# A fifth buffer of gathered rows in the residual's place, masks laid down before the scores, and two side products moved

## The chip, the cores and the metric

The kernel runs as one program on one core of a Trainium2 chip. The time is the device time of one execution in microseconds (us). Before the change it is 2636.42 us, the median of 3 runs (2633.18 to 2641.44). Five engines work side by side and wait for each other by semaphores: TensorE (PE: matmuls and transposes into PSUM; its weight loads are shown as PEld), VectorE (DVE), ScalarE (ACT), GpSimd (POOL) and SyncE (SP). Here SP issues the loads of weights and POOL the gathers and stores.

## The reference, cut to what matters

Two layers of a decoder for 512 prompt tokens and 8 sampled sequences of 4 tokens. The sampled tokens attend over a paged cache of 2048 old rows per sequence, in three branches that share the queries:

```
kv_c, ends = compress_kv(cmp_all, w_cmp1, w_cmp2)        # blocks of 32 rows -> one key and value
o_cmp, p_cmp = cmp_attend(q, kv_c, ends, q_pos, ...)     # softmax over the compressed blocks
idx = select_blocks(p_cmp, q_pos, n_keys)                # top 16 of 33 blocks of 64 rows
o_slc = sel_attend(q, idx, q_pos, blocks, slopes)        # softmax over rows of the selected blocks
o_win = win_attend(q, keys, q_pos, k_pos, slopes)        # softmax over the last 512 rows
o_a = ga[0] * o_cmp + ga[1] * o_slc + ga[2] * o_win
x = x + mix @ w_out                                      # x: the residual, needed again only here
```

A softmax score is `q.k - slope * distance`, with blocked rows at minus infinity. The rest of a layer (input projection, prompt attention, gated linear attention, mixing, ConvFFN) is not touched.

## The kernel before, in words

All is in fp32. The residual rows lie turned in SBUF (`xT`, 128 x 8 x 544) for the whole program. In a layer the normed rows `hT` are made from `xT`; after that `xT` is not read until the products `wo0` to `wo7` are added to it (DVE, L2189), some 700 us into a layer of 1300 us.

Past rows come in pieces of 2 MB, one for each sequence and branch (128 partitions x 16 rows x 256 numbers). POOL issues them (`gather`, L687; `window`, L695) into `XSLOTS` = 4 buffers, taken in turn in the order of `XSTEPS`: `cmp0` to `cmp8`, `win0`, `slc0` to `slc3`, `win1`, `slc4` to `slc7`. A piece may start when the last user of the piece four places earlier is done (`x_slot_free`). So `slc3` takes the buffer of `win0` and waits for its last product (`ow0`), `win1` takes that of `slc0` and waits for the last product of the first half (`os0`), and `slc7` takes that of `win1` and waits for `ow1`. POOL's queue is in order: whatever stands behind a waiting gather waits too.

Sampled attention is done in two halves of 4 sequences, each one PE, DVE and ACT in turn:

- window: keys turned (L989), scores (L996), mask distances added and the maximum taken (DVE), exponentials (ACT), probabilities turned (L1007, L1008), times values (L1015, L1019);
- selected rows: keys turned in four steps (L1057), each copied out of PSUM by ACT and DVE, scores in four steps (L1068) into two PSUM pairs `ss..0` and `ss..1`; DVE adds the distances `dslc` to each pair (1024 wide), then over all 2048 the selection mask `selml`, takes the maximum over 2080, ACT takes exponentials over 2080, PE turns the probabilities (L1086, L1090), and multiplies by the values (L1100, L1104).

Where a softmax chain runs, PE is given a piece of the input projection that needs nothing from it, 32 matmuls of 272 columns at L790: a side product. `side_steps` says where: `("s", 0, 2)` (`qb0`) behind the first window scores, `("s", 0, 0)` (`qb1`) behind the first half's selected scores, `("s", 1, 1)` (`kb0`) ahead of the second window, `("s", 1, 0)` (`kb1`) behind the second half's selected scores. DVE copies each out of PSUM. PE and DVE use two PSUM pairs in turn (`T0`, `T1`) for turned tiles and side products.

## Time and profile before

| | |
|---|---|
| runs, median (lowest to highest) | 2636.42 us (2633.18 to 2641.44) |
| profiled execution, own time | 2633.0 us |
| its span | 2630.7 us |
| PE busy | 2474.3 us, 94% of the span |
| DVE busy | 794.6 us, 30% |
| ACT busy | 525.1 us, 20% |
| mean granted clock of PE | 0.957 of full speed |

PE is the busiest engine and 87% of the chain that ended last. A line number such as L1650 can be that of a helper (here the DVE copy, L1641 the DVE tensor-tensor operation, L1367 every ACT operation), so instructions are told apart by their tiles and widths. The granted clock has two levels, 1.00 and 0.50 of full speed. The first layer spans about 20 to 1321 us of the trace; sampled attention lies at 239 to 363 us, and again 1300 us later in the second layer.

### The profile page before, as it was taken

The page shows a single profiled execution, that of the slowest core. Times are in us where ns is not written, and L with a number is a line of the kernel's source. Part 1 is how long each engine was busy: PE and PEld are TensorE (multiplying, and loading weights), DVE is VectorE, ACT ScalarE, POOL GpSimd, SP SyncE. Part 2 cuts the span into 40 slices and gives each one's busy share as a digit, 9 for nine tenths or more (in the row PEclk, how much of TensorE's full clock was granted, in tenths as well). Part 3 has the DMA queues.
Part 4 walks back from the last instruction along what each step waited for, and adds up shares of the span by engine and source line. Part 5 has one row for each costly group of instructions (what it writes and reads, how often), then busy time and mean ns, then how long its engine had stood idle before and what let it go on. Part 6 is the DMA issues. An engine that isn't in the chain of part 4 may idle for free.

```text
span 2630.7 us, 31111 instructions
## 1 busy us (share of the span) xinstructions
PE 2474.3 (94%) x13222; PEld 1994.0 (76%) x13222; DVE 794.6 (30%) x1829; ACT 525.1 (20%) x1067; POOL 97.0 (4%) x182
## 2 busy tenths in 40 slices
PE   7999789999998999999999987999999989999998
PEld 5787567678887888888877865766788878888886
DVE  2444333642412112210015543356431122112001
ACT  1254111550101111110012531135310011111100
POOL 3010000000000000000000100000000000000000
PEclk8998899997999999999999978999989999999999
DMA  6444421111221222222262534211112212221222
GB/s 194 126 170 176 186 71 49 33 33 35 64 83 48 64 80 64 81 57 67 73 209 91 202 144 177 65 49 25 27 48 80 67 48 80 64 81 59 64 72 67
DMA packets 184576, 228.52 MB, mean 87 GB/s; under 512 B 37470, under 2 KB 170932, under 8 KB 180084
## 3 DMA queue, kind: packets, MB, share of 16 engines
q1 hardware_dynamic: 174008, 133.11, 17.2%
q0 software_dynamic: 10432, 93.44, 9.4%
q8 instruction: 105, 1.72, 0.3%
q14 instruction: 31, 0.25, 0.0%
HBM read 218.19 MB, written 16.66 MB: 89 GB/s over the span
## 4 chain that ended last, share of the span: by engine, by line
PE 87%; DVE 7%; DMA 2%; ACT 2%; issue 1%; DVEq 0%; SPq 0%; POOLq 0%; ACTq 0%
PE PS L790 50%; PE PS L1336 12%; PE PS L812 5%; PE PS L909 4%; DVE arena L1650 3%; PE PS L897 2%; ACT arena L1367 2%; PE PS L1141 1%; DMA arena<-in_cache_kv_slc_dram,idx 1%; PE PS L1152 1%; PE PS L1057 1%; PE PS L433 1%; DVE arena L1641 1%; PE PS L1254 1%; DMA arena<-in_state_kv_win_dram 1%
## 5 line engine op out<-in xcount | busy, mean ns | idle before, releaser
L790 PE MATMUL PS<-hT,ring 128*128 128x272 f32 x4608 | 1081.0, 397 | 14.0 <-DVE hT L1647 10.7
L790 PEld LDWEIGHTS PS<-hT,ring 128*128 128x128 f32 x4608 | 882.4, 192 | 208.6 <-issue 25.9
L1367 ACT ACTIVATE arena<-PS 64x512 f32<-64x512 f32 (+10 forms) x480 | 241.9, 525 | 1295.3 <-PE PS L790 709.7
L1336 PE MATMUL PS<-arena,ring 128*128 128x272 f32 x1408 | 323.5, 393 | 1.9 <-DVEq L2225 1.9
L1336 PEld LDWEIGHTS PS<-arena,ring 128*128 128x128 f32 x1408 | 267.2, 190 | 57.6 <-DVEq L2225 2.7
L1650 DVE COPY arena<-PS 64x512 f32<-64x512 f32 (+6 forms) x215 | 155.8, 726 | 323.3 <-PE PS L790 103.1
L1641 DVE TENSOR_TENSOR arena<-PS,arena 128x544 f32<-128x544 f32 (+3 forms) x120 | 73.1, 621 | 418.9 <-PE PS L790 399.5
L790 PE MATMUL PS<-arena,ring 128*128 128x272 f32 x768 | 177.2, 393 | 3.1 <-DVE arena L1641 3.1
L1647 DVE SCALAR_TENSOR_TENSOR arena<-arena,prm 128x32 f32<-128x32 f32 (+1 forms) x176 | 87.9, 500 | 291.2 <-ACT arena L1367 288.1
L790 PEld LDWEIGHTS PS<-arena,ring 128*128 128x128 f32 x768 | 145.8, 190 | 33.9 <-DVE arena L1641 4.0
L1641 DVE TENSOR_TENSOR xT<-PS,xT 128x544 f32<-128x544 f32 x32 | 23.2, 724 | 427.0 <-PE PS L1336 319.1
L812 PE MATMUL PS<-ring,hT 128*128 128x256 f32 x640 | 140.8, 381 | 0.6 <-ACT qT L1367 0.6
L909 PE MATMUL PS<-arena 128*128 128x256 f32 (+1 forms) x576 | 134.9, 378 | 5.8 <-ACT arena L1367 3.4
L812 PEld LDWEIGHTS PS<-ring,hT 128*128 128x128 f32 x640 | 120.8, 190 | 19.4 <-issue 1.6
L909 PEld LDWEIGHTS PS<-arena 128*128 128x128 f32 x576 | 101.6, 194 | 23.3 <-issue 6.8
L1367 ACT ACTIVATE arena<-xT 128x544 f32<-128x544 f32 x40 | 25.5, 654 | 414.4 <-DVE xT L1641 414.1
L1367 ACT ACTIVATE arena<-arena 128x544 f32<-128x544 f32 (+6 forms) x110 | 71.4, 673 | 103.6 <-DVE arena L1641 64.7
L1367 ACT ACTIVATE arena<-arena,small 128x128 f32<-128x128 f32 (+3 forms) x128 | 70.6, 556 | 25.1 <-DVE small L1647 24.7
L897 PE MATMUL PS<-ident,arena 128*128 128x128 f32 (+1 forms) x576 | 73.1, 271 | 0.3 <-DVE kv_kT L1650 0.3
L790 PE MATMUL PS<-qT,ring 128*128 128x272 f32 x256 | 69.9, 435 | 0.0
L897 PEld LDWEIGHTS PS<-ident,arena 128*128 128x128 f32 (+1 forms) x576 | 64.2, 142 | 7.2 <-issue 1.1
L1057 PE MATMUL PS<-ident,arena 128*128 128x128 f32 x256 | 43.9, 341 | 27.0 <-DMA arena<-in_cache_kv_slc_dram,idx 27.0
(278 smaller groups left out, 1644.9 us busy)
## 6 DMA issues: line engine op xcount, KB each, us to landing
ring<-in_w_up_dram SPq DMA_DIRECT2D x88, 512.0 KB, 4.6
ring<-in_w_in_dram SPq DMA_DIRECT2D x68, 512.0 KB, 4.7
ring<-in_w_down_dram SPq DMA_DIRECT2D x32, 384.0 KB, 3.8
ring<-in_w_down_dram SPq DMA_DIRECT2D x32, 320.0 KB, 4.4
arena<-in_state_kv_win_dram POOLq DMA_DIRECT2D x4, 2048.0 KB, 15.7
ring<-in_w_out_dram SPq DMA_DIRECT2D x16, 512.0 KB, 4.5
out_dram<-in_state_kv_win_dram POOLq DMA_DIRECT2D x2, 4064.0 KB, 22.7
ring<-in_w_in_dram SPq DMA_DIRECT2D x16, 256.0 KB, 4.8
```

The source lines that it names most:

```text
L433: mm = pe.matmul(PS[HD * g:HD * g + HD, VBANKS[qt % 2], P * r:P * r + P], kv[:, t, 1 + br, P + HD * g:P + HD * g + HD], PTp[j % 2][:, g, P ...
L790: mm = pe.matmul(PS[0:m, b + a, 0:HALF], weight(k), rhs(k)[:, HALF * a:HALF * a + HALF], start=(k == 0), stop=(k == nk - 1))
L812: mm = pe.matmul(out, hT[:, k, P * t:P * t + nt], w[:, k, c0:c0 + n], start=(k == 0), stop=(k == KC - 1))
L897: mm = pe.transpose(PS[:, b + r // 4, P * (r % 4):P * (r % 4) + n], XB[s][0:n, 8 * q + r, P * c:P * c + P], ident[0:n, 0:n])
L909: mm = pe.matmul(out, w1[:, c, 4 * q + pr, :, :], XT[j % 2][:, pr, :, 0:n], start=(q == 0 and pr == 0), stop=(q == 1 and pr == 3))
L1057: mm = pe.transpose(PS[:, b + i, P * m:P * m + P], XB[s][:, 4 * j + m, 0:P], ident[:, :])
L1141: mm = pe.matmul(PS[:, b + g, 0:P * (qt + 1)], qT[HD * g:HD * g + HD, r, P * qt:P * qt + P], kT[HD * g:HD * g + HD, br, 0:P * (qt + 1)], s ...
L1336: mm = pe.matmul(PS[:, b + a, 0:HALF], w[:, k, :], aT[:, 11 * half + k, HALF * a:HALF * a + HALF], start=(half == 0 and k == 0), stop=(hal ...
L1367: return nc.scalar.activation(out, in_, func, **kw)
L1641: return nc.vector.tensor_tensor(out, a, b_, op)
L1647: return nc.vector.scalar_tensor_tensor(out=out, in0=a, scalar=s_, in1=b_, op0=op0, op1=op1)
L1650: return nc.vector.tensor_copy(out, a)
```

## The change

1. `XSLOTS` becomes 5. The fifth buffer is the first 4096 columns of `xT`. POOL stores all of `xT` to memory (into the places of `y_p` and `y_s`, which are written with the result only at the very end) once all of `hT` is made, waits for that store, gathers `cmp4` into the place, and after `ow1` brings `xT` back. DVE waits for it (`x_back`) ahead of the `wo` adds. `win0` and `win1` now use this fifth buffer, `slc3` that of `cmp8`, and `slc4` to `slc7` those of `slc0` to `slc3`.
2. The masks of the selected scores are laid into the score buffer `z` ahead of the scores: `z = selml + dslc` over 2048, and the scores of the new rows and their maximum, before the keys are copied. Scores are then added and the maximum taken in one instruction for each 1024 (`tensor_tensor_reduce`), and only three maxima are left to join. The same for the window (512 wide).
3. The window of the first half is taken earlier: its probabilities are turned ahead of `imp`, and its values multiplied ahead of `oc`. It has a buffer of its own (`ptnw`) for the turned new rows.
4. Side products: `qb0` moves from behind the first window scores to behind `oc`, ahead of the first keys; `kb1` moves from behind the second half's selected scores to ahead of its keys.
5. The values product starts its first 8 rows once `pt..0` is copied, rather than `pt..0`, `pt..1` and `ptn` all.

```diff
-XSLOTS = 4
+XSLOTS = 5
-    at = dict(zip((("s", 0, 2), ("s", 0, 0), ("s", 1, 1), ("s", 1, 0)), SIDE))
+    at = dict(zip((("s", 0, 2), ("s", 0, 0), ("s", 1, 1), ("s", 1, 2)), SIDE))
-        XOFF, TOFF = 0, XSLOTS * 4096
+        XOFF, TOFF = 0, (XSLOTS - 1) * 4096
+        xrows = xT[:, :, :].rearrange("p k n -> p (k n)")
+        XB = [carve(4096 * i, STRIDE, 256) for i in range(XSLOTS - 1)] + [xrows[:, 0:4096].rearrange("p (l c) -> p l c", c=256)]
+        x_away = [(xrows[:, 0:4096], y_p.rearrange("o (p a) d -> p (o a d)", a=4)),
+                  (xrows[:, 4096:KC * NT], y_s.rearrange("b t (q n) -> (b t q) n", n=256))]
...
# POOL
                 for b in range(4):
                     gather(f"cmp{b}", ins["cache_kv_cmp"], b)
+                gp.wait_ge(*S.at(gp, "h_ready", KC))
+                for rows, place in x_away:
+                    gp.dma_start(place, rows).then_inc(*S.inc(gp, "x_stored", 16))
+                gp.wait_ge(*S.at(gp, "x_stored"))
+                gather("cmp4", ins["cache_kv_cmp"], 4)
                 gp.wait_ge(*S.at(gp, "kv_ready"))
...
+                gp.wait_ge(*S.filled(gp, "ow1"))
+                for rows, place in x_away:
+                    gp.dma_start(rows, place).then_inc(*S.inc(gp, "x_back", 16))
                 for s in range(XSLOTS):
...
# PE, sampled attention
                 window_scores(0)
-                side(("s", 0, 2))
+                window_probabilities(0)
                 pe.wait_ge(*S.at(pe, "pc_s", 1))
...
                 mm.then_inc(*S.fill(pe, "pcT"))
+                window_values(0)
                 pe.wait_ge(*S.drained(pe, "pcT"))
...
                         window_scores(hf)
-                    window_values(hf)
+                        window_probabilities(hf)
+                        window_values(hf)
+                    side(("s", hf, 2))
...
-                    pe.wait_ge(*S.drained(pe, f"pt{hf}0"))
-                    pe.wait_ge(*S.drained(pe, f"pt{hf}1"))
-                    pe.wait_ge(*S.drained(pe, f"ptn{hf}"))
                     for i in range(STRIDE):
+                        if i % 8 == 0:
+                            pe.wait_ge(*S.drained(pe, f"pt{hf}{i // 8}"))
...
# DVE, selected rows of a half
+                    tt(z4, bc(selml[:, :, :].unsqueeze(3), [P, STRIDE, NSEL - 1, 4]),
+                       bc(dslc[:, :].rearrange("p (s f) -> p s f", f=4).unsqueeze(1), [P, STRIDE, NSEL - 1, 4]), ALU.add).then_inc(*S.inc(dv, "dve_step"))
+                    copy(z[:, 2048:2048 + NS], snew[:, hf, :])
+                    rmax(small[:, 98:99], snew[:, hf, :]).then_inc(*S.inc(dv, "dve_step"))
+                    side_copy(("s", hf, 2))
                     turned_keys(dv, copy, hf, 0, 1)
...
-                        tt(z[:, 1024 * lg:1024 * lg + 1024].rearrange("p (m n) -> p m n", m=8), PS[:, b:b + 2, :].rearrange("p a (m n) -> p (a m) n", m=4),
-                           bc(dslc[:, :].unsqueeze(1), [P, 8, P]), ALU.add).then_inc(*S.drain(dv, f"ss{hf}{lg}"))
-                    copy(z[:, 2048:2048 + NS], snew[:, hf, :])
-                    tt(z4, z4, bc(selml[:, :, :].unsqueeze(3), [P, STRIDE, NSEL - 1, 4]), ALU.add).then_inc(*S.inc(dv, "dve_step"))
-                    rmax(small[:, 22:23], z[:, :]).then_inc(*S.inc(dv, "dve_step"))
-                    tsc(small[:, 32:33], small[:, 22:23], nslope_c, ALU.mult).then_inc(*S.inc(dv, "nb_s"))
+                        zl = z[:, 1024 * lg:1024 * lg + 1024]
+                        nc.vector.tensor_tensor_reduce(zl, PS[:, b:b + 2, :].rearrange("p a n -> p (a n)"), zl, 1.0, -3e38, ALU.add, ALU.max,
+                                                       small[:, 96 + lg:97 + lg]).then_inc(*S.drain(dv, f"ss{hf}{lg}"))
+                        if lg == 0:
+                            tt(small[:, 98:99], small[:, 98:99], small[:, 96:97], ALU.max).then_inc(*S.inc(dv, "dve_step"))
+                    tsc(small[:, 32:33], small[:, 97:98], small[:, 98:99], ALU.max, nslope_c, ALU.mult).then_inc(*S.inc(dv, "nb_s"))
...
                 dv.nop().then_inc(*S.inc(dv, "arena_ffn"))
+                dv.wait_ge(*S.at(dv, "x_back"))
                 for m in range(KC):
                     dv.wait_ge(*S.filled(dv, f"wo{m}"))
```

The order of instructions, first on POOL from the store of new compressed rows to the end of the gathers, before (names: `kv_kT` holds the new keys and values, `arena` the four buffers, `out_dram` the outputs):

```order
L703 DMA out_dram<-kv_kT 128x4x256 [waits kv_ready]
L687 DMA arena<-in_cache_kv_cmp_dram,idx 128x4096 [waits filled_T0] x4
```

and now, from the store of the residual, with the same lines a few numbers on:

```order
L708 DMA out_dram<-xT 128x4096 [waits h_ready]
L708 DMA out_dram<-xT 128x256
L691 DMA xT<-in_cache_kv_cmp_dram,idx 128x4096 [waits x_stored,layer_done]
L713 DMA out_dram<-kv_kT 128x4x256 [waits kv_ready]
L691 DMA arena<-in_cache_kv_cmp_dram,idx 128x4096 [waits filled_T0] x3
```

The store of the residual and a wait for it now stand ahead of the store of new rows, and one gather moved ahead with them. The end of the same queue, before:

```order
L695 DMA arena<-in_state_kv_win_dram 128x4x1024 [waits filled_T0]
L687 DMA arena<-in_cache_kv_slc_dram,idx 128x4096 [waits filled_T0] x3
L687 DMA arena<-in_cache_kv_slc_dram,idx 128x4096 [waits filled_S1]
L695 DMA arena<-in_state_kv_win_dram 128x4x1024 [waits filled_S0]
L687 DMA arena<-in_cache_kv_slc_dram,idx 128x4096 [waits filled_S0] x4
L729 TENSOR_SCALAR idx<-idx 128x8 [waits x_in0,x_in1,x_in2,x_in3]
```

and now:

```order
L699 DMA xT<-in_state_kv_win_dram 128x4x1024 [waits filled_T0]
L691 DMA arena<-in_cache_kv_slc_dram,idx 128x4096 [waits filled_T0] x4
L699 DMA xT<-in_state_kv_win_dram 128x4x1024 [waits filled_S0]
L691 DMA arena<-in_cache_kv_slc_dram,idx 128x4096 [waits filled_S0] x4
L739 DMA xT<-out_dram 128x4096 [waits filled_S0]
L739 DMA xT<-out_dram 128x256
L743 TENSOR_SCALAR idx<-idx 128x8 [waits x_in0,x_in1,x_in2,x_in3,x_in4]
```

The fourth gather of the first half no longer waits for a `filled_S` semaphore (a values product) but for `filled_T0` (the last turned compressed rows), and all four of the second half stand behind one wait.

PE in the second half, from the first half's last product to the first turned keys, before (L790 is a side product, `x_in` semaphores are gathered pieces):

```order
L1104 MATMUL PS<-kv_kT,arena 32x128 x4
L790 MATMUL PS<-hT,ring 128x272 [waits drained_T1,w_in1]
L790 MATMUL PS<-hT,ring 128x272 x15
L989 MATMUL PS<-ident,arena 128x128 [waits drained_T0,x_in2]
L989 MATMUL PS<-ident,arena 128x128 x7
L989 MATMUL PS<-ident,arena 128x128 [waits drained_T1]
L989 MATMUL PS<-ident,arena 128x128 x7
```

```order
L1015 MATMUL PS<-arena 32x128 [waits drained_T0,drained_S0]
L1015 MATMUL PS<-arena 32x128 x15
L1019 MATMUL PS<-kv_kT,arena 32x128 x4
L1057 MATMUL PS<-ident,arena 128x128 [waits x_in3,drained_T1]
L1057 MATMUL PS<-ident,arena 128x128 x3
L1057 MATMUL PS<-ident,arena 128x128 [waits x_in0]
```

and now:

```order
L804 MATMUL PS<-hT,ring 128x272 [waits drained_T1,w_in1]
L804 MATMUL PS<-hT,ring 128x272 x15
L1003 MATMUL PS<-ident,xT 128x128 [waits drained_T0,x_in4]
L1003 MATMUL PS<-ident,xT 128x128 x7
L1003 MATMUL PS<-ident,xT 128x128 [waits drained_T1]
L1003 MATMUL PS<-ident,xT 128x128 x7
L1010 MATMUL PS<-arena,qbd 32x512 [waits drained_T1,drained_T0,drained_S1]
L1010 MATMUL PS<-arena,qbd 32x512 x3
```

```order
L1033 MATMUL PS<-xT,arena 32x128 [waits drained_T0,drained_S0]
L1033 MATMUL PS<-xT,arena 32x128 x15
L1037 MATMUL PS<-kv_kT,arena 32x128 x4
L804 MATMUL PS<-hT,ring 128x272 [waits drained_T1,w_in1]
L804 MATMUL PS<-hT,ring 128x272 x15
L1077 MATMUL PS<-ident,arena 128x128 [waits x_in0,drained_T0]
L1077 MATMUL PS<-ident,arena 128x128 x3
L1077 MATMUL PS<-ident,arena 128x128 [waits x_in1]
```

The side product `kb1` (L804, second piece) now stands between the window's values and the first turned keys.

DVE in the second half, from the selection mask on, before (L1641 adds, L1650 copies, L1656 takes a maximum):

```order
L1641 TENSOR_TENSOR arena<-selm,l_row 128x512 [waits drained_S0]
L1650 COPY arena<-PS 128x1024 [waits filled_T0,dve_step]
L1650 COPY arena<-PS 128x1024 [waits filled_T0,filled_S0]
L1650 COPY arena<-PS 128x1024 [waits filled_T0,kt_used]
L1641 TENSOR_TENSOR arena<-PS,dslc 128x1024 [waits filled_S1]
L1650 COPY arena<-PS 128x1024 [waits filled_T0,filled_S1]
L1641 TENSOR_TENSOR arena<-PS,dslc 128x1024 [waits filled_S0]
L1650 COPY arena<-arena 128x32 [waits drained_S0,drained_S1]
L1641 TENSOR_TENSOR arena<-arena 128x2048
L1656 TENSOR_REDUCE small<-arena 128x1 [waits dve_step]
L1644 TENSOR_SCALAR small<-small,cols 128x1 [waits dve_step]
```

and now (the ISA rows at L1974 are the fused add and maximum, and the reading of its result):

```order
L1662 TENSOR_TENSOR arena<-selm,l_row 128x512 [waits drained_S0]
L1662 TENSOR_TENSOR arena<-arena,dslc 128x2048 [waits dve_step]
L1671 COPY arena<-arena 128x32
L1677 TENSOR_REDUCE small<-arena 128x1
L1671 COPY kbT<-PS 128x544 [waits filled_T1]
L1671 COPY arena<-PS 128x1024 [waits filled_T1,dve_step]
L1671 COPY arena<-PS 128x1024 [waits filled_T1,filled_S0]
L1671 COPY arena<-PS 128x1024 [waits filled_T1,kt_used]
L1974 ISA arena,small<-PS,arena 128x1024 [waits filled_S1]
L1974 ISA small 128x1
L1662 TENSOR_TENSOR small<-small 128x1 [waits drained_S1]
L1671 COPY arena<-PS 128x1024 [waits filled_T1,filled_S1,dve_step]
```

The add over 2048 moved from behind the scores to ahead of the first copied keys, and the maximum over 2080 is gone.

## Rows read from the trace of the kernel before

**Rows 1.** Busy time by stretch: the two halves of layer 0.
```profile
core 0: us, PE busy (x) PEld busy (x) DVE busy (x) ACT busy (x) POOL busy (x), PEclk, DMA share, GB/s
239.00:303.10 64.10, 49.13 (x408) 36.30 (x408) 30.05 (x73) 13.21 (x20) 0.94 (x1) 0.77 0.14 50
...
303.10:363.40 60.30, 42.90 (x386) 31.75 (x382) 21.66 (x36) 10.31 (x13) 4.80 (x6) 0.86 0.49 192
```

**Rows 2.** Waits of PE on transfers, both layers: total us, times, longest.
```profile
PE PS L1057 <- DMA arena<-in_cache_kv_slc_dram,idx: 27.0, 6, 7.5
```

**Rows 3.** GpSimd's timeline, layer 0: start us, us, what [idle before <-releaser].
```profile
51.20 0.94 POOL L687 DMA_INDIRECT arena<-in_cache_kv_cmp_dram,idx  x1 [0.30 <-issue]
...
120.18 0.82 POOL L703 DMA_DIRECT2D out_dram<-kv_kT  x1 [68.04 <-DVEq L1764]
...
173.33 0.94 POOL L687 DMA_INDIRECT arena<-in_cache_kv_cmp_dram,idx  x1 [11.19 <-PE PS L897]
...
230.93 0.94 POOL L687 DMA_INDIRECT arena<-in_cache_kv_slc_dram,idx  x1 [8.14 <-PE PS L897]
...
265.18 0.94 POOL L687 DMA_INDIRECT arena<-in_cache_kv_slc_dram,idx  x1 [33.31 <-PE PS L1019]
...
303.76 0.79 POOL L695 DMA_DIRECT2D arena<-in_state_kv_win_dram  x1 [37.64 <-PE PS L1104]
...
307.36 0.94 POOL L687 DMA_INDIRECT arena<-in_cache_kv_slc_dram,idx  x1 [0.31 <-issue]
...
325.12 0.93 POOL L687 DMA_INDIRECT arena<-in_cache_kv_slc_dram,idx  x1 [16.82 <-PE PS L1019]
```

**Rows 4.** Timeline of the first half of layer 0, all engines.
```profile
248.92 8.79 PE L790 MATMUL PS<-hT,ring 128*128 128x272 f32 x32
...
273.98 4.53 PE L1057 MATMUL PS<-ident,arena 128*128 128x128 f32 x20 [6.89 <-DMA arena<-in_cache_kv_slc_dram,idx]
...
275.19 1.22 DVE L1650 COPY arena<-PS 128x1024 f32<-128x1024 f32 x1 [8.39 <-PE PS L1057]
...
286.85 7.60 PE L790 MATMUL PS<-hT,ring 128*128 128x272 f32 x32
...
286.98 1.23 DVE L1641 TENSOR_TENSOR arena<-PS,dslc 128x1024 f32<-128x1024 f32 x1 [1.27 <-PE PS L1068]
...
288.40 2.28 DVE L1641 TENSOR_TENSOR arena<-arena 128x2048 f32<-128x2048 f32 x1
...
290.71 2.32 DVE L1656 TENSOR_REDUCE small<-arena 128x1 f32<-128x2080 f32 x1
...
293.32 2.12 ACT L1367 ACTIVATE arena<-arena,small,cols 128x2080 f32<-128x2080 f32 x1 [8.70 <-DVE small L1644]
...
295.58 1.97 PE L1086 MATMUL PS<-ident,arena 128*128 128x128 f32 x16 [1.14 <-ACT arena L1367]
...
299.07 3.70 PE L1100 MATMUL PS<-arena 128*32 128x128 f32 x128 [0.99 <-DVE arena L1650]
```

**Rows 5.** Timeline of the second half of layer 0, PE.
```profile
312.12 1.97 PE L989 MATMUL PS<-ident,arena 128*128 128x128 f32 x16 [1.47 <-DMA arena<-in_state_kv_win_dram]
...
319.55 1.08 PE L1007 MATMUL PS<-ident,arena 128*128 128x128 f32 x4 [2.99 <-ACT arena L1367]
...
328.13 1.09 PE L1057 MATMUL PS<-ident,arena 128*128 128x128 f32 x4 [1.95 <-DMA arena<-in_cache_kv_slc_dram,idx]
...
333.72 3.83 PE L1057 MATMUL PS<-ident,arena 128*128 128x128 f32 x20 [4.50 <-DMA arena<-in_cache_kv_slc_dram,idx]
...
354.55 1.97 PE L1086 MATMUL PS<-ident,arena 128*128 128x128 f32 x16 [1.14 <-ACT arena L1367]
```

**Rows 6.** Busy time by stretch (columns as rows 1): end of a window, two us later on.
```profile
257.30:264.00 6.70, 4.86 (x69) 3.47 (x67) 4.78 (x23) 1.13 (x3) 0.00 (x0) 0.82 0.01 2
...
324.00:326.00 2.00, 2.00 (x16) 1.57 (x8) 1.44 (x6) 0.00 (x0) 0.88 (x1) 0.50 0.81 336
```

**Rows 7.** DMA issues: KB each, us to landing.
```profile
out_dram<-arena SPq DMA_DIRECT2D x1, 2048.0 KB, 6.8
```

**Rows 8.** VectorE timeline, prompt attention: the fused add and maximum.
```profile
548.94 0.68 DVE L2016 CUSTOM_DVE_ANT_0 arena<-PS,dtab 128x512 f32<-128x512 f32 x1
```

41 lines of the change are left out of this document (21 added, 20 removed).

## The prediction

> **What bounds the kernel now.** I read the page first: PE is busy 94% of the span and holds 87% of the chain that ended last, so an edit pays where it shortens PE's idle time or raises PE's clock, and nowhere else. The change touches only sampled attention, so next I took busy time by stretch [rows 1]. In the first half of layer 0 PE is busy 49.1 of 64.1 us at a mean clock of 0.77, in the second 42.9 of 60.3 us at 0.86. Elsewhere PE is nearly full. The second layer repeats this 1300 us later, so I work out one layer and double it. Idle time here is 15.0 + 17.4 = 32.4 us a layer, which is the most that waits alone can give back.
>
> Then the waits of PE on transfers [rows 2]: 27.0 us in six waits of the turned selected keys (L1057), both layers together. In layer 0 they are three: 6.9, 1.95 and 4.5 us ahead of the matmuls at 273.98, 328.13 and 333.72 [rows 4, 5]. The second window waits 1.5 us more for its rows, at 312.12 [rows 5]. GpSimd's timeline says why [rows 3]: `slc3` is issued only at 265.18, after idling 33.3 us for L1019 (the window's values), and is used at 273.98, 8.8 us later; `win1` only at 303.76 (behind L1104) and used at 312.12; `slc7` only at 325.12 (behind L1019 again) and used at 333.72. Three times a layer a 2 MB piece is asked for just when it is wanted.
>
> The other idle times are softmax chains. In the selected rows, DVE after the last scores does an add of 1.23, one of 2.28 and a maximum of 2.32 us, and ACT 2.12 us of exponentials [rows 4]. From the end of the scores (286.9) to the turned probabilities (295.58) it is 8.7 us, of which a side product covers 7.6, and 1.1 is left. In the second half the same again: the add that starts the chain follows scores that end at 345.9, and L1086 starts at 354.55 [rows 5].
>
> **The fifth buffer.** `slc3` takes the buffer of `cmp8`, free at 230.9, where `slc2` is issued before. Transfers wanted at once land in 8.8 us, so it lands by about 241 and is wanted after 264: this wait goes. `win1` may load from `ow0` on, 45 us ahead of use: this wait goes. `slc4` to `slc7` start behind `os0`, as `win1`, `slc4` to `slc6` did: those four were issued from 303.76 to 307.36 and the last was usable at 328.13 [rows 3, 5], 24.4 us after the first issue. So `slc7` can be used at about 328.1. What now takes 24 us of PE ahead of it is side product `kb0`, the window and side product `kb1`, below.
>
> The new transfers: the store of 2.2 MB is bounded by the store of the result, the same size, 6.8 us [rows 7], and stands behind four gathers issued by 51.20 [rows 3]. Four 2 MB pieces took 24.4 us above, so the store lands near 52 + 24 + 7 = 83 us, and `cmp4` near 92. POOL's queue behind it wants nothing before 120.18 [rows 3]: 28 us of cover after `cmp4` has landed. `cmp4` itself is wanted when four pieces are turned, which is when POOL gets the fourth buffer back, at 173.33 [rows 3]. I cost it at nothing. The way back is issued behind `slc7`; it lands in the 330s and DVE wants it near 750 us.
>
> **First half, new order.** Window scores end at 249.0 as before. The fused add and maximum at 512 takes 0.68 us [rows 8] and one small reading of 0.1; with 0.2 for the scaling, ACT starts at 250.1 and PE turns the probabilities at 251.1 (in the second half before, ACT's part takes 1.0 us). Then, all at half clock: five transposes 1.3, `imp` 0.6, a copy by ACT and `pcT` 0.8, values 2.5, `oc` 0.6, to 256.9. These instructions stood between 257.3 and 264.0 before, 4.9 us of work in 6.7 [rows 6], where they waited for the copy of `qb0` and for the selection; I count 5.8. DVE's chain behind `imp` (selection, output adds, `selml`) moved with it, from 266.8 to near 261.4 at its end. The add of 2048 is laid behind it, 2.28 us [rows 4], with 0.4 for copy and maximum of the new rows: 264.1. Meanwhile `qb0` runs from 256.9: 7.57 us at full clock, 8.79 at the head of a cold stretch [rows 4]; I take 8.0, so 264.9. The cover holds by 0.8 us; without it the 2.7 us of DVE would be on PE's path. Two groups of turned keys (1.0 each at full clock, the second behind the copy of `qb0`, 0.7) bring the DVE copy that was at 275.19 [rows 4] to 267.0. Gain 8.2. This one term holds the whole wait of 6.9 and what the window chain gives.
>
> From that copy to the end of the scores it was 11.7 us (275.19 to 286.9) in the first half, which starts at half clock, and 10.9 in the second. PE now comes warm out of `qb0`: gain 0.7. Then the chain behind the scores: the fused instruction at 1024 is in no trace; its bounds are 1.23 us, the plain add of that width, and 1.23 + 1.2 (half of the 2.32 us maximum) if it went twice over the data [rows 4]. At 512 the fused one (0.68) costs no more than the plain one does (0.69), so I take 1.3 with its reading. With 0.25, then 2.12 and 0.2 on ACT, the chain is 4.1 us instead of 8.7, and `qb1` (7.6) covers it: gain 1.1, not 4.6. Last, the values product (L1100) starts 1.0 us after its wait on the DVE copy [rows 4]; it now starts behind `ptn`: gain 0.9. Sum of the first half: 8.2 + 0.7 + 1.1 + 0.9 = 10.9 us.
>
> **Second half, new order.** `kb0` ends at 310.7. The window's keys start there and not at 312.12, but the second group waits for the copy of `kb0` (to 311.5): they end at 312.8, not 314.1, gain 1.3. Fused add and maximum: 0.9. The values end at 322.1 instead of 324.3. Now `kb1`, 7.6 us plus some 0.9 because the clock is at 0.50 there [rows 6]: 330.6. DVE's mask work (1.1 + 0.7 + 2.3 + 0.4 = 4.5 us) is under it. Keys are copied by DVE at 332.7, not 334.9: gain 2.2, and this is all that is left of 4.5 + 1.95 + 1.4 + 0.9 us, since 7.6 us of product were put in. The data of `slc7` was there at 328.1, used at 331.7: margin 3.6 us.
>
> Behind the scores nothing covers the chain now: 4.1 us bare, against 8.7 before: gain 4.6. But PE stands idle for 4 us. After 3.0 us of idle ahead of L1007 [rows 5] the clock is at 0.50, and still is at 324 to 326 [rows 6]; the turned probabilities are 1.97 us for 16 at full clock [rows 5] and twice that at half. I take 2.0 off; the least is 0, the most 2.0 + 1.9 (half of L1100 too). The Trainium skill (TensorE: Matmul & The Clock Gate, part 1) says that the half clock is the resting state and a stretch of work lifts it; this speaks against uncovering the chain, and the rows agree: by the rule as by the rows 2 us of the 4.6 go. The values product again 0.9. Sum of the second half: 2.2 + 4.6 - 2.0 + 0.9 = 5.7 us.
>
> **The sum.** 16.6 us a layer, 33 us in two. 2633.0 - 33 = 2600 us for the profiled execution; the median of the runs shown is 3.4 us above it, and I give 2602. Least: the fused instruction at 2.5 (2 us more in the second half, less where covered), no gain of the clock, 3.9 off: 12 a layer, 2611. Most: clock warm throughout (2.0 + 0.9 + 0.4 more): 20 a layer, 2595.
>
> **Rivals.**
>
> A, the transfers come late. The way back of `xT` is issued at about 322, while `slc6` and `slc7` are in flight; it moves 2.2 MB, and one 2 MB piece of four in 24.4 us is 6 us. If it shares the engines evenly, `slc7` lands up to 6 us later, at 334, against 331.7: 2.3 us and a cold clock after it, 2 more; with the gathers' own spread 4 to 5 us a layer, total 2611. For: the engines are full there (the gathers of that stretch). Against: in rows 3 and 5 pieces became usable in the order of issue. The Trainium skill (DMA: Bandwidth & Descriptors, "Two DMAs through the same engine are not ordered") says that in one queue of an engine descriptors start in order though they overlap; by this the way back costs nothing, and the sum stays 2602. By its fit for such a transfer (2.0 us plus bytes over 436 per ns), an estimate, four pieces land in 21 us, where the trace has 24.4.
>
> B, the clock stays up. If fewer idle gaps keep PE at full clock through both windows and the bare chain, the penalties go (2.0, 0.9, and 0.4 of `qb0`): 3.3 us a layer more, 2595. Against: the first half's window begins at half clock already, and 4 us bare is longer than the 3.0 us after which it fell.
>
> C, slower. POOL's queue stands still until the residual's store has landed, and the store of new rows, `cmp5` and all behind it wait. `cmp4` is wanted at 173 [rows 3] and lands 8.8 us after its issue, so PE starts to wait when the store lands after 164 us, 81 us later than I reckon; the change is slower once that excess passes 17 us a layer, from a landing at 181 us on. With 25 us of excess in each layer it would be 2636 + 2 x (25 - 16.6) = 2653. Nothing in the rows shows a store of 2 MB over 7 us [rows 7].
>
> D, it does not do what it says: some other wait takes the place of the fifth buffer and only the chains' gain stays (1.1 + 0.9 + 4.6 - 2.0 + 0.9 = 5.5 a layer): 2624. The order shows no such wait.
>
> **How the numbers follow.** Forecast 30 to 36 us less: 0.58. A: 0.20. B: 0.15. D: 0.04. C: 0.03. A change under 0.3% (8 us) cannot be told from none in these runs. Faster: 0.96; same 0.02; slower 0.02. The range 2590 to 2615 takes in A, B and the least and most above.
>
> **What would show it.** Right: no wait of PE on a gathered piece at the selected keys; first half (window keys to last values) near 53 us instead of 64, second near 54 instead of 60; `slc3` issued by 232, `slc4` to `slc7` together; a bare gap of 4 us ahead of the second turned probabilities with the clock at 0.50 behind it; about 1.3 us for the fused instruction. Wrong: PE waiting for `x_in` in the second half (A), no 0.50 behind the bare gap (B), POOL idle on the store past 120 us (C), stretches outside sampled attention that got longer.

## The result, and the profile after

The changed kernel takes 2597.89 us (median of 4 runs, 2596.63 to 2600.86), the one before, run beside it, 2638.39 us (4 runs, 2633.18 to 2641.44): ratio 0.985, 95% interval 0.983 to 0.987. The forecast was 2602 with a range of 2590 to 2615. By the medians that is 40.5 us less, where the forecast had 34 (2636.4 to 2602). The profiled execution took 2596.85 us, its span is 2595.0 us (2630.7 before), the mean granted clock 0.962. PE is busy 95% of the span and holds 89% of the chain that ended last, transfers 0%.

Busy time of the two halves of layer 0, against [rows 1] (same columns; the first stretch begins 1.6 us ahead of the window's first turned keys, as that of [rows 1] does):

```profile
237.55:289.08 51.53, 44.63 (x408) 32.87 (x408) 27.46 (x77) 13.21 (x20) 0.79 (x1) 0.85 0.18 62
289.08:341.78 52.70, 43.56 (x386) 32.45 (x382) 18.06 (x35) 10.31 (x13) 5.17 (x7) 0.87 0.55 222
```

The first half takes 51.5 us instead of 64.1 (53 forecast), the second 52.7 instead of 60.3 (54 forecast). PE's mean clock rose from 0.77 to 0.85 in the first half and hardly changed in the second, 0.86 and 0.87. Of the waits of PE (total, times, longest), the one on gathered pieces [rows 2] is gone, and the two softmax chains head what belongs to this stage, window (L1021) and selected rows (L1106):

```profile
PE PS L1021 <- ACT arena L1387: 8.3, 4, 2.1
PE PS L1106 <- ACT arena L1387: 7.8, 2, 3.9
```

GpSimd's timeline, against [rows 3]:

```profile
75.57 1.00 POOL L691 DMA_INDIRECT xT<-in_cache_kv_cmp_dram,idx  x1 [25.91 <-DMA out_dram<-xT]
...
229.31 0.94 POOL L691 DMA_INDIRECT arena<-in_cache_kv_slc_dram,idx  x1 [8.16 <-PE PS L911]
254.77 0.79 POOL L699 DMA_DIRECT2D xT<-in_state_kv_win_dram  x1 [24.52 <-PE PS L1037]
289.99 0.96 POOL L691 DMA_INDIRECT arena<-in_cache_kv_slc_dram,idx  x1 [34.44 <-PE PS L1124]
...
308.06 1.14 POOL L739 DMA_DIRECT2D xT<-out_dram  x2 [13.38 <-PE PS L1037]
314.17 0.24 POOL L743 TENSOR_SCALAR idx<-idx 128x8 int32<-128x8 int32 x1 [4.96 <-DMA arena<-in_cache_kv_slc_dram,idx]
```

`slc3` is issued at 229.31, some 34 us ahead of use, `win1` at 254.77. POOL resumes at 314.17, when `slc7` has landed: 24.2 us after the first of the four was issued, 24.4 before, and that with the way back issued at 308.06. The residual's store had landed at 75.5.

The first half on PE and DVE, against [rows 4]:

```profile
252.47 1.31 PE L1033 MATMUL PS<-xT,arena 128*32 128x128 f32 x32
...
254.64 7.60 PE L804 MATMUL PS<-hT,ring 128*128 128x272 f32 x32
...
264.63 1.23 DVE L1671 COPY arena<-PS 128x1024 f32<-128x1024 f32 x1 [1.25 <-PE PS L1077]
...
275.29 7.60 PE L804 MATMUL PS<-hT,ring 128*128 128x272 f32 x32
...
275.42 1.22 DVE L1974 CUSTOM_DVE_ANT_0 arena<-PS,arena 128x1024 f32<-128x1024 f32 x1 [1.27 <-PE PS L1088]
276.57 0.08 DVE L1974 DVE_READ_ACCUMULATOR2_ANT small<- 128x1 f32 x1
```

The fused instruction takes 1.22 us and 0.08 for its reading. The window's values begin cold and take 1.31 us, where they take 1.93 when all is cold (below): the clock rose inside them. The second half on PE, against [rows 5]:

```profile
296.51 2.14 PE L1003 MATMUL PS<-ident,xT 128*128 128x128 f32 x16
...
303.22 0.66 PE L1021 MATMUL PS<-ident,arena 128*128 128x128 f32 x4 [2.09 <-ACT arena L1387]
...
304.91 1.93 PE L1033 MATMUL PS<-xT,arena 128*32 128x128 f32 x32 [0.93 <-ACT arena L1387]
...
307.35 9.39 PE L804 MATMUL PS<-hT,ring 128*128 128x272 f32 x32
316.59 3.25 PE L1077 MATMUL PS<-ident,arena 128*128 128x128 f32 x24
...
333.39 3.68 PE L1106 MATMUL PS<-ident,arena 128*128 128x128 f32 x16 [3.90 <-ACT arena L1387]
...
337.21 4.22 PE L1119 MATMUL PS<-arena 128*32 128x128 f32 x128
```

No transfer is waited for. `kb1` costs 9.39 us instead of 7.60, the turned probabilities behind the bare gap 3.68 instead of 1.97, the values 4.22 instead of 3.70. The clock by windows (columns as [rows 1]) around these:

```profile
307.40:311.00 3.60, 3.60 (x12) 2.79 (x9) 3.26 (x7) 0.00 (x0) 1.14 (x2) 0.50 1.01 428
333.00:336.00 3.00, 2.61 (x12) 2.61 (x13) 0.00 (x0) 0.94 (x3) 0.00 (x0) 0.50 0.00 0
```

### The profile page after: what moved, and what is told of

Same layout as the page of the kernel before. It is cut to its first block, busy times and chain, and to the rows that moved or that the text cites. A ratio compares the mean times of both kernels' runs of the same rounds, so it can differ in the third digit from the quotient of the medians.

```text
span 2595.0 us, 31135 instructions
## 1 busy us (share of the span) xinstructions
PE 2468.7 (95%) x13222; PEld 1987.7 (77%) x13222; DVE 784.7 (30%) x1845; ACT 525.1 (20%) x1067; POOL 102.3 (4%) x190
## 4 chain that ended last, share of the span: by engine, by line
PE 89%; DVE 7%; ACT 2%; issue 1%; DMA 0%; DVEq 0%; SPq 0%; ACTq 0%
PE PS L804 52%; PE PS L1356 12%; PE PS L826 5%; PE PS L923 4%; DVE arena L1671 3%; PE PS L911 2%; ACT arena L1387 2%; PE PS L1161 1%; PE PS L1172 1%; PE PS L437 1%; PE PS L1077 1%; PE PS L1274 1%; DVE arena L1662 1%; PE PS L1119 1%; DVE arena L1702 1%
## 5 line engine op out<-in xcount | busy, mean ns | idle before, releaser
L804 PE MATMUL PS<-hT,ring 128*128 128x272 f32 x4608 | 1085.7, 398 | 14.0 <-DVE hT L1668 10.7
L804 PEld LDWEIGHTS PS<-hT,ring 128*128 128x128 f32 x4608 | 885.6, 193 | 206.4 <-issue 22.2
L804 PE MATMUL PS<-arena,ring 128*128 128x272 f32 x768 | 177.2, 393 | 3.2 <-DVE arena L1662 3.2
L804 PEld LDWEIGHTS PS<-arena,ring 128*128 128x128 f32 x768 | 145.8, 190 | 33.9 <-DVE arena L1662 4.0
L804 PE MATMUL PS<-qT,ring 128*128 128x272 f32 x256 | 70.5, 437 | 0.0
L911 PE MATMUL PS<-ident,arena 128*128 128x128 f32 (+1 forms) x512 | 65.4, 272 | 0.0
L804 PEld LDWEIGHTS PS<-qT,ring 128*128 128x128 f32 x256 | 53.7, 214 | 14.0 <-issue 1.7
L1172 PEld LDWEIGHTS PS<-ident,arena 128*128 128x128 f32 x320 | 34.3, 142 | 37.9 <-issue 23.1
```

What stands on the lines that cost most here:

```text
L804: mm = pe.matmul(PS[0:m, b + a, 0:HALF], weight(k), rhs(k)[:, HALF * a:HALF * a + HALF], start=(k == 0), stop=(k == nk - 1))
L911: mm = pe.transpose(PS[:, b + r // 4, P * (r % 4):P * (r % 4) + n], XB[s][0:n, 8 * q + r, P * c:P * c + P], ident[0:n, 0:n])
L1172: mm = pe.transpose(PS[:, b, P * t:P * t + P], ex[j % SLOTS][:, g, P * t:P * t + P], ident[:, :])
```

## The measure for the experiments

The runs of one kernel scatter by 4 us and more; the stage scatters less (211.1 and 211.2 us in two profiles of the changed kernel), though it is read from a single profiled execution of each kernel, and the two layers of one execution differ in it by up to 2.7 us (only_fifth). So each trace is also read by stretches: "first" from the products of the new rows to the end of the first half's last values product, "second" from there to the end of the second half's, both layers added, and "rest" the other 2380 us of the span.

| kernel | runs, median (lowest to highest) | ratio to before, 95% | first | second | rest |
|---|---|---|---|---|---|
| before | 2638.39 (2633.18 to 2641.44) | | 131.1 | 117.6 | 2382.0 |
| changed | 2597.89 (2596.63 to 2600.86) | 0.983 to 0.987 | 106.1 | 105.0 | 2383.9 |
| changed_again | 2596.36 (2593.62 to 2600.62) | 0.983 to 0.986 | 106.1 | 105.1 | 2383.2 |
| four_buffers | 2598.24 (2596.02 to 2599.37) | 0.983 to 0.986 | 105.9 | 107.0 | 2381.2 |
| only_fifth | 2604.04 (2602.61 to 2607.30) | 0.985 to 0.989 | 112.4 | 105.3 | 2382.8 |
| masks_late | 2605.17 (2604.28 to 2605.63) | 0.985 to 0.989 | 108.2 | 114.5 | 2381.0 |
| late_values | 2600.65 (2596.58 to 2608.67) | 0.984 to 0.989 | 109.5 | 110.8 | 2376.9 |
| kb1_behind | 2591.34 (2590.26 to 2595.69) | 0.981 to 0.984 | 106.1 | 101.9 | 2381.8 |
| fill_gap | 2593.93 (2589.52 to 2598.32) | 0.982 to 0.985 | 106.1 | 101.4 | 2384.0 |
| fill_all | 2582.56 (2581.65 to 2584.89) | 0.978 to 0.981 | 104.3 | 95.5 | 2380.0 |
| four_fill | 2587.55 (2585.27 to 2592.31) | 0.979 to 0.982 | 104.5 | 105.2 | 2380.7 |
| kb1_fill | 2594.65 (2591.81 to 2605.30) | 0.982 to 0.987 | 104.3 | 103.7 | 2381.8 |
| fill_more | 2581.29 (2581.11 to 2584.39) | 0.977 to 0.980 | 101.4 | 95.5 | 2382.5 |

In the stage the change took 37.6 us off, where the forecast had 33. The rest moved by up to 7 us between kernels that are the same there. The reason is seen in layer 1 of two of them, 75 to 95 us behind sampled attention, the same work at nearly the same time. The changed kernel, then four_buffers, by windows:

```profile
1691.00:1701.00 10.00, 7.11 (x57) 4.04 (x57) 7.03 (x36) 4.55 (x19) 0.00 (x0) 0.96 0.34 105
1701.00:1711.00 10.00, 10.00 (x38) 5.72 (x35) 4.21 (x27) 3.69 (x20) 0.00 (x0) 0.53 0.01 2
```

```profile
1691.00:1701.00 10.00, 7.11 (x59) 4.08 (x58) 6.87 (x35) 4.38 (x18) 0.00 (x0) 1.00 0.35 107
1701.00:1711.00 10.00, 10.00 (x58) 7.28 (x55) 4.21 (x28) 3.93 (x20) 0.00 (x0) 1.00 0.00 0
```

After the same short idle times PE goes on at 0.53 in the one and at 1.00 in the other, which costs the changed kernel 4.6 us here (PE is through with the product that follows at 1716.2 and at 1711.8, and was 0.2 ahead). Such a dip is there or not in a layer; a difference of less than 5 us between two medians says little by itself, and I go by the stage. The changed kernel's profile has such a dip in both layers, that of before in layer 0 alone. The rest of the span is 1.9 us longer in the changed one, so the span fell by 35.7 and not by 37.6; what else moved in the rest was not sought.

## Experiments

### Is it the fifth buffer?

four_buffers:

```diff
-XSLOTS = 5
+XSLOTS = 4
-                for rows, place in x_away: ...            # store and way back gone
-                gp.wait_ge(*S.at(gp, "x_stored"))
-                dv.wait_ge(*S.at(dv, "x_back"))
```

> The changed kernel with four buffers again: no store and no way back of the residual, the gathers in the old turn. Masks, window order, side products and values product stay as changed. Theory 1 (the fifth buffer and the new order hide the same transfers, so either alone gives most): slc3 is issued when ow0 is done, near 254 us, lands 8.8 us later near 263, and its rows are wanted at 263.4: no wait, or under 1 us. win1 is issued at the end of the first half (289) and lands at 298 where the changed kernel turns its keys at 296.5: 1.3 us lost. slc7 is issued at ow1 (near 308) and lands near 317, under kb1, which ends at 316.6 plus 1.3: nothing. With 1 us for a colder clock that is 2 to 3 us a layer: 2601 to 2605. Theory 2 (the fifth buffer carries the gain, the waits on gathered pieces come back as they were, 27 us of them in both layers plus the windows' 3): 2620 to 2628.

only_fifth: the kernel before, with these lines added and nothing else of the change.

> The kernel before with the fifth buffer alone (five buffers, residual stored and brought back, gathers in the new turn); masks, chains, side products as before. Theory 1: the wait of 6.9 us in the first half goes, in the second half slc4 to slc7 are issued together and slc7 is there 24.3 us after, where it was used 30.7 us after the half began: 6 us. 13 us a layer, some 26 in all: 2610 to 2614, and with the result of the kernel with four buffers the two parts overlap (each alone gives more than its share). Theory 2 (gains add up, the chains and the order give 5.5 us a layer as the rival D of the prediction put it): 2638 minus 29 = 2609, with four buffers at 2627. So this one alone can't tell them apart, the pair can. Rival: the store and the way back cost something themselves, then slower than 2614.

Measured: four_buffers 2598.24, stage 212.9 against 211.1 of the changed kernel: without the fifth buffer 35.8 of 37.6 us stay. only_fifth 2604.04, stage 217.8: the fifth buffer alone takes 30.9 off. The two don't add up (35.8 + 30.9 against 37.6): they hide the same transfers, theory 1. Both medians lie below what theory 1 gave (2601 to 2605, and 2610 to 2614). For only_fifth the missing part is in the first half, 9.3 us a layer where I had the wait of 6.9 alone. From the window's last product to the first scores it was 14.2 us before (264.27 to 278.43) and is now 4.9 (264.54 to 269.41): besides the wait, 2.4 us of slow turned keys behind it are gone. And the fifth buffer alone doesn't end the waits, since `slc7` is still late in the second half of only_fifth:

```profile
319.12 4.02 PE L1070 MATMUL PS<-ident,arena 128*128 128x128 f32 x20 [2.62 <-DMA arena<-in_cache_kv_slc_dram,idx]
```

PE in four_buffers (first the issue of `slc7` and the wait for it on POOL):

```profile
309.60 0.94 POOL L691 DMA_INDIRECT arena<-in_cache_kv_slc_dram,idx  x1 [15.88 <-PE PS L1027]
319.19 0.24 POOL L733 TENSOR_SCALAR idx<-idx 128x8 int32<-128x8 int32 x1 [8.64 <-DMA arena<-in_cache_kv_slc_dram,idx]
```

```profile
297.46 1.97 PE L993 MATMUL PS<-ident,arena 128*128 128x128 f32 x16 [1.39 <-DMA arena<-in_state_kv_win_dram]
...
308.69 8.61 PE L794 MATMUL PS<-hT,ring 128*128 128x272 f32 x32
317.14 3.31 PE L1067 MATMUL PS<-ident,arena 128*128 128x128 f32 x24
```

`win1` is late by 1.4 us, as worked out. `slc7` lands 9.6 us after its issue, behind a `kb1` of 8.6 and twelve turned keys: no wait. In the first half `slc3` is issued at 254.55 and is just in time as well, since `qb0` (254.21 to 261.8) now stands between window and keys. I read that from these rows; no run puts `qb0` alone back in its old place.

### The masks, the values, the place of kb1

masks_late:

```diff
-                    tt(z4, bc(selml...), bc(dslc...), ALU.add)       # ahead of the keys, with copy and maximum of the new rows
...
-                        nc.vector.tensor_tensor_reduce(zl, PS[:, b:b + 2, :].rearrange("p a n -> p (a n)"), zl, 1.0, -3e38, ALU.add, ALU.max,
+                        tt(z[:, 1024 * lg:...], PS[...], bc(dslc...), ALU.add)
...
+                    tt(z4, z4, bc(selml...), ALU.add)
+                    rmax(small[:, 22:23], z[:, :])
```

> The changed kernel with the masks of the selected scores added after the scores, over 2048, and the maximum over 2080 taken after that, as before (the window's fused operation stays). Theory: the bare chain of the second half is 8.7 us again instead of 4.0, 4.6 more; in the first half 7.6 of 8.7 are covered, 1.1 more; the turned probabilities behind the gap are at half clock in either case. 5.7 us a layer, 2598 + 11 = 2609. Rival 1: DVE's early mask work (2.3 us) delayed the keys, so that part comes back in the first half: 2605 to 2607. Rival 2: the longer idle makes the clock stay low longer behind it (values product and later), 2 us a layer more: 2613.

Measured: 2605.17, stage 11.6 us longer (2.1 in the first halves, 9.5 in the second), that is 5.8 a layer against 5.7: the theory. The first halves' 2.1 are the 1.1 a layer expected there, so rival 1 is out, though the median fell into its range: it moved by 7.3 only, since the rest of the span is 2.9 shorter. The idle time ahead of the second half's turned probabilities is 9.03 us instead of 3.90:

```profile
340.64 3.67 PE L1106 MATMUL PS<-ident,arena 128*128 128x128 f32 x16 [9.03 <-ACT arena L1387]
```

Behind it the 16 take 3.67 us, no more than behind 3.90; the values then take 4.75 instead of 4.22. In layer 1 there is not even that: behind 8.67 us of idle time the values are at full speed:

```profile
1626.81 3.53 PE L1106 MATMUL PS<-ident,arena 128*128 128x128 f32 x16 [8.67 <-ACT arena L1387]
...
1630.38 3.70 PE L1119 MATMUL PS<-arena 128*32 128x128 f32 x128
```

So rival 2, a longer slow stretch behind a longer idle time, is out too.

late_values:

```diff
-                        if i % 8 == 0:
-                            pe.wait_ge(*S.drained(pe, f"pt{hf}{i // 8}"))
+                    pe.wait_ge(...)      # pt0, pt1 and ptn ahead of the first row
```

> The changed kernel with the values product of the selected rows waiting for all three copies of turned probabilities again. Theory: in each half the product starts behind DVE's copy of the second 1024 and ACT's copy of the new rows, 0.9 us later: 1.8 us a layer, 3.6 in all, 2601.5. Rival: the copies are long done by the time that PE has turned the new rows (half clock makes this slower in the second half), so nothing in the second half: 1.8 in all, 2599.7.

Measured: 2600.65, stage 9.2 us longer, where 3.6 was expected. The median is near the 2601.5 expected by luck: this profile has no dip in either layer, and its rest is 7 us shorter. PE in its second half:

```profile
335.69 3.68 PE L1106 MATMUL PS<-ident,arena 128*128 128x128 f32 x16 [3.90 <-ACT arena L1388]
...
340.89 5.28 PE L1120 MATMUL PS<-arena 128*32 128x128 f32 x128 [1.30 <-DVE arena L1672]
```

The wait is 1.30 us, and the values then take 5.28 instead of 4.22: here an idle time of a microsecond in a stretch at half clock cost as much again in clock. Of the first half's 2.2 us in layer 0, 1.15 are the wait; the others lie ahead of the edit, in a window that stayed cold through its values (1.94 instead of 1.31), so they aren't its doing. In both layers together some 7 us of the 9.2 are the edit's: waits of 1.15 and 1.3 and 1.1 of clock in each. What the forecast missed is the clock, and 0.65 us a layer of the waits.

kb1_behind:

```diff
-... ("s", 1, 1), ("s", 1, 2)), SIDE))
+... ("s", 1, 1), ("s", 1, 0)), SIDE))
```

> The changed kernel with side product kb1 behind the selected scores of the second half again, and so none in front of the keys. Theory 1: PE is through with the window at 307.4 and then waits for slc7, which lands at 314.2 whatever PE does; the keys start 2.4 us earlier than at 316.6, but cold (1 to 2 us back); behind the scores kb1 (7.6 us) covers the chain of 4 us and keeps the clock up, where the changed kernel had 3.9 idle and 2.2 of half clock: 7.6 - 6.1 = 1.5 more. Together 0 to +1.5 us a layer: 2598 to 2601, not to be told from the changed kernel by much; so placing kb1 in front gives nothing beside a fifth buffer. Rival: the uncovered chain was the bigger mistake, this kernel faster than the changed one by 3 or more: 2592 to 2595. Rival 2: without 7.6 us of cover slc7 costs 6 us a layer: 2608 or more.

Measured: 2591.34, the stage 3.1 us shorter, all of it in the second halves. That is the first rival and not theory 1. PE in its second half:

```profile
308.63 2.82 PE L1077 MATMUL PS<-ident,arena 128*128 128x128 f32 x12
315.59 4.32 PE L1077 MATMUL PS<-ident,arena 128*128 128x128 f32 x20 [4.13 <-DMA arena<-in_cache_kv_slc_dram,idx]
...
328.19 7.60 PE L804 MATMUL PS<-hT,ring 128*128 128x272 f32 x32
335.63 2.07 PE L1106 MATMUL PS<-ident,arena 128*128 128x128 f32 x16
```

I had let all keys wait for `slc7`; twelve of 32 are turned before. Counted from the start of the half (290.4 here, 289.1 in the changed kernel), the rest begin at 25.2 us, while `kb1` in the changed kernel lasts to 27.5 with all keys still to come. The scores end 2.5 us earlier here. Behind them 7.6 us of `kb1` cover the chain and keep the clock, and from there to the end it takes 1.5 us more, as expected. So the 9.4 us of `kb1` in front bought nothing.

### Is it the clock?

fill_gap, and in it nothing that is computed changes (the transposes go where the turned probabilities go next):

```diff
                     side(("s", hf, 0))
-                    pe.wait_ge(*S.at(pe, "es", 2 * hf + 2))
                     for a in range(2):
...
+                        if a == 0:
+                            if hf:
+                                for i in range(28):
+                                    pe.transpose(PS[:, b + i // 4 % 2, ...], ident[:, :], ident[:, :])
+                            pe.wait_ge(*S.at(pe, "es", 2 * hf + 2))
```

> The changed kernel with 28 transposes of the identity in the bare gap ahead of the second half's turned probabilities, into the PSUM banks that these overwrite; nothing computed changes. At full clock 28 take 3.5 us of the 3.9 idle. Theory (the clock falls because PE is idle there): the 16 turned probabilities take 1.97 us instead of 3.68, the values product 3.70 instead of 4.22: 2.2 us a layer, 4.5 in all, ratio to the changed kernel 0.998, about 2593.5; and the granted clock is 1.00 in the window behind. Rival (the half clock has another cause, or the extra transposes run over the gap): no change, or 1 to 2 us longer.

fill_all has the same loop with 8 and 15 ahead of the windows' turned probabilities and 7 ahead of the second window's values.

> fill_gap, and transposes of the identity in the gaps of both windows too: 8 ahead of the first window's turned probabilities, 15 ahead of the second's, 7 ahead of its values. Theory: in addition kb1 takes 7.6 instead of 9.4, the second window's values 1.3 instead of 1.93, in the first window 0.3: 2.7 us a layer beyond fill_gap, some 2588. Rival: in the first window, which begins at half clock, 8 transposes take 2.0 us at that clock and delay what follows by up to 1 us; then equal to fill_gap within 2 us.

fill_more has 4, 4 and 6 more in the first window, ahead of its turned keys and its scores, and claims the banks of the scores earlier for it.

> fill_all, and 4, 4 and 6 transposes more in the three gaps of the first window ahead of its turned keys and its scores (0.9, 1.1 and 1.4 us; all three fit even at half clock). Theory: this stretch is at half clock from its start because of the gaps ahead of it; with fewer gaps the clock rises some us sooner, so that up to 1.0 (second eight turned keys) and 0.9 (scores) and 0.5 (values) come back: 1 to 2.4 us a layer, 2578 to 2581. Rival: the clock doesn't rise sooner, for it also stays at half through gaps that are only part filled: 2582.6, no change.

Measured: fill_gap 2593.93 (expected 2593.5), stage 3.6 us shorter (4.5 expected); fill_all 2582.56 (2588 expected), stage 11.3 us shorter (9.9 expected), the rest another 3.9; fill_more 2581.29, first halves 2.9 us shorter again, though its median can't be told from that of fill_all. PE in the second half of fill_all:

```profile
301.75 1.86 PE L1020 MATMUL PS<-ident 128*128 128x128 f32 x15
303.90 0.66 PE L1023 MATMUL PS<-ident,arena 128*128 128x128 f32 x4 [0.30 <-ACT arena L1395]
...
305.51 1.08 PE L1037 MATMUL PS<-xT,arena 128*32 128x128 f32 x32
...
306.87 7.60 PE L804 MATMUL PS<-hT,ring 128*128 128x272 f32 x32
...
327.15 3.28 PE L1111 MATMUL PS<-ident 128*128 128x128 f32 x28
331.12 1.97 PE L1114 MATMUL PS<-ident,arena 128*128 128x128 f32 x16 [0.69 <-ACT arena L1395]
...
333.54 3.70 PE L1127 MATMUL PS<-arena 128*32 128x128 f32 x128
```

Each of the four slow groups is back at its full speed: values 1.08 (1.93), `kb1` 7.60 (9.39), turned probabilities 1.97 (3.68), values of the selected rows 3.70 (4.22). Idle time of PE became useless work and nothing that is computed was changed, so these 4.8 us a layer (105.0 less 95.5, halved) were the clock's. The first window stays at half clock in fill_all through its scores (1.94); with fill_more the second eight keys take 1.50 and the scores 1.06. The Trainium skill (TensorE: Matmul & The Clock Gate, part 1) says that a stretch of work lifts the clock from its resting level; these two rows of fill_more agree, against 1.97 and 1.93 in the changed kernel.

### With the clock up, what are the fifth buffer and kb1's place worth?

four_fill is four_buffers with the loops of fill_all; kb1_fill is kb1_behind with them and 54 transposes ahead of `slc7`'s keys.

> The kernel with four buffers (no store, no way back of the residual) with the same transposes of the identity in its gaps as fill_all: 8, 15 and 7 in the windows, 28 ahead of the second half's turned probabilities. Theory: the fifth buffer is worth nothing to the changed kernel, because PE's half clock there (window values, kb1 9.4) hid the time that transfers need; with the clock up they are late: win1 by 1.4 us, slc7, which took 9.6 us from its issue at ow1, by some 0.7 behind a kb1 of 7.6. With a cold stretch behind one of them 2 to 3.5 us a layer against fill_all: 2587 to 2590. Rival: even then nothing waits long enough, equal to fill_all, 2582.6 within 2 us; the fifth buffer is then superfluous.

> kb1 behind the selected scores, with the transposes of fill_all in the windows and 54 more (6.3 us at full clock) in PE's wait for slc7, which ends 24.3 us after the issue of slc4 whatever PE does. Theory (what made kb1_behind faster than the changed kernel is only the clock): with the clock up in both orders, kb1 in front wins, since behind the scores 7.6 us cover a chain of 4: second half 49.5 us instead of fill_all's 47.8; 2 us a layer slower than fill_all, some 2586. Rival: kb1 behind is better in itself: below 2582.

Measured: four_fill 2587.55, in the expected range and 5 us above fill_all. Its stage is 9.8 us longer, but the profiled execution took 2592.31, the longest of its five, and that of fill_all the shortest of its own; so the fifth buffer is worth some 5 to 10 us here. `win1` is late as it was in four_buffers, and now `slc7` is too:

```profile
299.14 1.97 PE L993 MATMUL PS<-ident,arena 128*128 128x128 f32 x16 [1.58 <-DMA arena<-in_state_kv_win_dram]
...
308.63 7.60 PE L794 MATMUL PS<-hT,ring 128*128 128x272 f32 x32
316.06 1.64 PE L1071 MATMUL PS<-ident,arena 128*128 128x128 f32 x12
319.91 4.07 PE L1071 MATMUL PS<-ident,arena 128*128 128x128 f32 x20 [2.21 <-DMA arena<-in_cache_kv_slc_dram,idx]
```

1.58 and 2.21 us of wait, and 1.6 of half clock behind the second. Both causes of the second are in the rows: `kb1` is 1.0 us shorter than in four_buffers (7.60 and 8.61), and `slc7` lands 1.0 us later after its issue (POOL resumes 10.6 us after it, 9.6 there). So a slow `kb1` hid a wait of some 1 us in four_buffers. Beside the new order the fifth buffer gives 1.8 us of the stage as PE runs there, and 5 or more once PE is not slowed.

kb1_fill: 2594.65, where 2586 was expected; second halves 103.7 against 95.5 of fill_all. The direction is the theory's, the size isn't:

```profile
310.07 0.63 PE L1083 MATMUL PS<-ident,arena 128*128 128x128 f32 x4 [2.33 <-DMA arena<-in_cache_kv_slc_dram,idx]
310.54 6.06 PE L1080 MATMUL PS<-ident 128*128 128x128 f32 x54
316.43 1.47 PE L1083 MATMUL PS<-ident,arena 128*128 128x128 f32 x12
```

PE waited 2.3 us for `slc6` first, which I had forgotten, and the 54 then ran to 316.43, past the landing of `slc7` (POOL resumed at 315.14). That is 1.3 us a layer of my own making; the other 2.8 (8.2 less 2.6, halved) are the order itself, by subtraction. It is not a clean measurement of the order: its sign stands, its size of some 3 us a layer does not.

### The store, and the changed kernel again

store_chain:

```diff
-                for rows, place in x_away:
-                    gp.dma_start(place, rows).then_inc(*S.inc(gp, "x_stored", 16))
+                for r in range(20):      # each waits for the one before
+                    for rows, place in x_away[0:1 if r < 19 else 2]: ...
```

> The changed kernel with the store of the residual's first 4096 columns done 20 times in a row, each waiting for the one before; the last one counts. The first landed at 75.5 us; at 6.8 us each the last lands near 205, cmp4 near 214, and PE wants it at 173.5. Theory (rival C's mechanism, its point of decision from 164 on): PE waits 40 us at the turned compressed rows of cmp4 in each layer, nothing before it, some 2598 + 80 = 2678. Rival: the stores disturb loads of weights and gathers, and PE loses time ahead of 173 us too; or less is lost, because work behind the gathers was not bound by them.

Measured: 2702.04 in a single run, where 2678 was expected. GpSimd, and the only wait of PE that is new:

```profile
222.54 0.99 POOL L691 DMA_INDIRECT xT<-in_cache_kv_cmp_dram,idx  x1 [6.70 <-DMA out_dram<-xT]
```

```profile
PE PS L912 <- DMA xT<-in_cache_kv_cmp_dram,idx: 98.7, 2, 59.1
```

The stores took up to 11 us each while other transfers ran and 6.8 towards the end of the chain, so the last landed at 221.4 and not at 205. PE waited 59.1 us in layer 0, until 232.15, and 39.6 in layer 1. The deadline follows: PE wants `cmp4` at 173.5 in the changed kernel, and it is usable 9.6 us after its issue, so POOL must have issued it by 163.9, with the store landed about a microsecond before (221.4 and 222.54 here); the forecast had 164 for the store. In the changed kernel `cmp4` is issued 88 us ahead of that.

> The changed kernel, unchanged, timed beside the next three on one chip: 2598 as before. Five of the kernels so far stood apart from their own stage times by up to 6 us, because the clock in the 50 to 100 us behind sampled attention is in some executions at 1.00 and in others at 0.90, for the same instructions; so its single runs should spread over 4 us or more, and its profile show one or both of the layers with that dip.

Measured: 2596.36, 2593.62 to 2600.62, and again the dip in both layers of its profile.

## Why the prediction was right

The time was right for the stage, 37.6 us against 33. The medians fell by 3 us more, and that lies outside the stage, in the scatter shown above; none of it was worked out.

- **The transfers.** Right as to what happens: no wait on gathered pieces, `slc7` 24.2 us after the first issue (24.4), nothing for the store (landed at 75.5, not 83) and the way back. Rival A and rival C are out by GpSimd's rows.
- **First half, 10.9 forecast, 12.5 measured.** The DVE copy came 9.1 us earlier, not 8.2, since the clock rose inside the window; keys and scores gave 1.0 (0.7), the chain behind them with the early values 2.4 (2.0). One cover was reckoned too well: the mask work was to end 0.8 us before `qb0`, but it ended 0.5 us after it (262.7 against 262.2), and PE waited 0.32 us for the copy of `qb0`, 0.65 in layer 1.
- **Second half, 5.7 forecast, 6.3 measured.** The copy of the keys came 2.2 us earlier, as worked out, though two errors cancel in it: the window ran warmer than thought (0.66 for its turned probabilities) and `kb1` took 9.4, not 8.5. The bare chain gave 4.8 (4.6). The turned probabilities lost 1.7 (2.0). The values lost 0.5 for the clock, which I had put only into the bounds, and won 1.4 of waits (0.9).
- **The fused instruction** was taken at 1.3 and is 1.22 and 0.08: once over the data.
- **What failed: rival D's price.** It said that without the fifth buffer's effect only the chains' 5.5 us a layer stay, 2624. four_buffers is 2598.24. The sum had put the whole wait of 6.9 us under the heading of the buffer while the same step (264.9 as the start of the keys, `qb0` in between) would have let `slc3` be in time without it: 254 + 8.8 = 263. I never asked which of the two hid the wait. The time came out right because the sum counted the wait once; the cause as told, "a fifth buffer", is not what carries this change. The order of the work carries it (35.8 us alone), and the buffer carries nearly as much alone (30.9). Of the order, the masks are worth 11.6 us and the early values some 7; `kb1` in front costs 3.1. What the move of `qb0` and the earlier window are worth one by one was not measured.
- **Rival B** did not come true, the clock fell behind the bare chain as the forecast had it. But what the clock costs was larger than the 3.3 us a layer that I gave it: filling the gaps brought 5.6 a layer (stage of fill_all).

Open: why the clock fell in some executions and not in others after the same idle times. That wasn't tried, and one such dip is worth some 4.6 us of a run.

## What to carry to other kernels

When a change both starts a transfer earlier and puts work in front of its use, work out each alone: they hide the same wait, and one may be free to drop. Before giving a side product to a transfer that is late, look at what clock it will run; here PE was slowed by its own gaps by more than any wait that was left, and 58 useless transposes a layer took 11.3 us off the stage and 15 off the median (2597.89 to 2582.56), the version to build on. Judge an edit worth under 5 us by its own stretch of the trace, in both layers, and mind which of the runs was profiled.
